# Decay levels of a gated linear recurrence: six levels in place of seven, products side by side in one bank, a compact matrix for the low levels

## The chip, the cores and the metric

The kernel runs on one core of a Trainium2 chip. The time is that of the device, in microseconds, from the launch on the core to its end; the median of several runs is compared. PE (TensorE) multiplies matrices and writes them to PSUM (8 banks, 512 fp32 columns of 128 partitions each); DVE (VectorE) and ACT (ScalarE) read and write PSUM and SBUF; POOL (GpSimd) works on SBUF alone; SP (SyncE) issues the DMAs. Each engine runs its own queue in order and waits on semaphores for the others.

## The reference

One decoder layer on x (1 x 1024 x 1024, fp32): RMSNorm, one input projection, two groups of token mixers (a gated linear recurrence and sliding-window attention), output projection into the residual, RMSNorm, SwiGLU FFN (1024 to 2816 to 1024). What the change touches is the recurrence, 4 heads of 128 key channels and 128 value channels:

```python
q = silu(q) * 128 ** -0.5;  f = lb + (1 - lb) * sigmoid(f_logit);  k = 1 - f;  logf = log(f)
def step(state, inp):                       # one chunk of tokens
    bcum = cumsum(gb, axis=2)               # decay sums, per channel
    diff = bcum[:, :, :, None, :] - bcum[:, :, None, :, :]
    decay = exp(where(causal, diff, NEG_INF))
    scores = einsum('bhtc,bhsc,bhtsc->bhts', qb, kb, decay)
    o_intra = einsum('bhts,bhsv->bhtv', scores, vb)
    o_inter = einsum('bhtc,bhcv->bhtv', qb * exp(bcum), state)
    btot = bcum[:, :, -1:, :]
    new_state = exp(btot[:, :, 0, :])[..., None] * state + einsum('bhsc,bhsv->bhcv', kb * exp(btot - bcum), vb)
    return new_state, o_intra + o_inter
o = rms_norm(o, out_gain) * silu(g)
```

The scores of a chunk carry a decay that depends on the channel, so they are no plain product of q and k.

## The kernel before

The tokens lie along the free dimension, channels on the partitions; a chunk is 128 tokens, 8 chunks (NC) a head. Projections and FFN are computed with each operand split in a high and a low part, three matmuls of 128x512 a step (the helper `three`, L1304 to L1306).

**The scores by levels.** The exponent b(t) - b(s) is written as (b(t) - m) - (b(s) - m), with m a decay sum between s and t, so that a product of q and k, each with its own factor, gives the score. One m doesn't serve all pairs, so there are 7 levels. At level lv, with L = 2^lv, a chunk falls into blocks of 2L tokens; m is the sum at the last token of the lower half; keys of the lower half meet queries of the upper half. Level 0 (L = 1) also gives the diagonal. A level goes through four engines:
- `LV` on POOL (L770): D = B - m, a subtraction of 128x1024; then `LV` on ACT (L1040, L1042 at level 0, else L1045 and L1046): the exponentials of both halves, in place
- `LX` on DVE (L1887): K times the factor, Q times the factor, into M, each 128x512 (L1875, L1878 at level 0, 128x1024 each)
- `LM` on PE (L1513): the products. Outputs are pieces of 32 partitions. Below 32 tokens only the four 32x32 pieces on a chunk's diagonal are computed (32 matmuls a level for the 8 chunks); at L = 32 there are 2 pieces of 32 columns a chunk, at L = 64 2 pieces of 64 columns. Each stands in PSUM at its place in the chunk's 128x128 score matrix, chunks 0 to 3 in bank 3, 4 to 7 in bank 4
- `LM` on DVE (L1897): two copies under a mask, 128x512 each, one a bank, that take what is valid at this level into the score matrix A (128 keys x 1024, fp32). The products of the next level wait for the copy of their bank

D and M have two buffers each, so `LV` of a level waits for the products two levels before, and `LX` for the matmuls two levels before.

Each matmul of fp32 shows as two records in the trace.

**Around the levels, per head.** `H1`: sigmoids and log on ACT. `HK`, `HQ`: K and Q on DVE. `HS` (L1854): the scan that gives the decay sums B. `H2`: exp(B) on ACT, its product with Q on POOL (L758), the tail difference on DVE (L1862) and its exponential on ACT; `HD` (L1867) multiplies it by K. `KT` (L1495): PE transposes that, into banks 3 and 4; `KE` on ACT copies it out. After the levels `OC`, chunk by chunk: a state product (L1528), the output product of A (L1530), the product with the state (L1533), and on DVE the state's update (L1906, L1910); ACT copies the outputs. `OS`, `OM`, `ON`, `OX` are the head's norm and gate. `W` (ACT, L942) and `WL` (DVE, L1739) split a projection weight tile in high and low; `MS`, `ML` split the input of the output projection.

**The order.** `schedule()` writes one list that all engines follow. `mix(dense, steps)` lays the steps of a head evenly between dense parts, each 6 matmuls of 128x512 of a projection. In head 0 there are 8 dense parts for the 7 levels, in heads 1 and 2 12 (2 more in head 2, of the output projection, for the last level), in head 3 16. Step lv of a head is `LM` of level lv, `LX` of lv + 2, `LV` of lv + 4.

## Time and profile before

| | us |
|---|---|
| median of 3 runs | 1136.88 (1135.83 to 1138.21) |
| the profiled execution | 1139.69 |
| its span, first to last instruction | 1138.0 |
| PE / DVE / ACT / POOL busy | 1093.1 / 699.3 / 497.3 / 439.4 |
| the four heads' levels and chunks | about 225 to 442 of the span |

The granted clock of TensorE is full (0.998 mean). A busy time counts the instructions' own time; the matmuls' ends are modelled and overlap, so that PE's rows are best read from start to start. An instruction's line names where it stands in the kernel; `x64` behind it counts records merged in one row. An idle time in brackets is the engine's own, just ahead of the instruction, with what ended it.

### The profile page before, as it was taken

How to read it: one execution, taken by the hardware profiler on the slowest of the kernel's cores; microseconds unless marked ns; L12 is line 12 of the kernel's file. 1: busy time of each engine (PE TensorE's matmuls, PEld its weight loads, DVE VectorE, ACT ScalarE, POOL GpSimd, SP SyncE). 2: the span in 40 equal slices, each digit the busy share in tenths (PEclk: the TensorE clock that was granted, in tenths of full speed). 3: DMA queues.
4: the chain of work that ended last, by engine and by line, in shares of the span. 5: the costliest groups of instructions: out<-in, count | busy, mean ns of one | idle time of the engine just before them, and what ended most of it. 6: DMA issues, size and time to landing. Idle time of an engine off the chain costs nothing.

```text
span 1138.0 us, 16737 instructions
## 1 busy us (share of the span) xinstructions
PE 1093.1 (96%) x6572; PEld 886.0 (78%) x6572; DVE 699.3 (61%) x884; ACT 497.3 (44%) x773; POOL 439.4 (39%) x351
## 2 busy tenths in 40 slices
PE   7999999979898999998999999999999999999998
PEld 7998766758676778776888888888888877788876
DVE  7205598596879897779332433243334497777776
ACT  8314466536456435454333333333333454454532
POOL 0301222354353332203646364536453844343462
PEclk9999999999999999999999999999999999999999
DMA  7101100010105104201333133313332594545333
GB/s 278 38 1 56 37 20 20 19 39 23 35 20 186 33 16 174 108 6 56 127 114 119 57 123 118 113 64 122 119 104 90 191 354 131 175 122 184 121 100 151
DMA packets 37102, 112.78 MB, mean 99 GB/s; under 512 B 4896, under 2 KB 9760, under 8 KB 35616
## 3 DMA queue, kind: packets, MB, share of 16 engines
q1 hardware_dynamic: 37024, 111.71, 28.5%
q8 instruction: 53, 0.87, 0.3%
q14 instruction: 25, 0.20, 0.1%
HBM read 83.12 MB, written 28.57 MB: 98 GB/s over the span
## 4 chain that ended last, share of the span: by engine, by line
PE 73%; DVE 12%; issue 5%; ACT 5%; POOL 3%; DMA 2%; SPq 0%; DVEq 0%; ACTq 0%; POOLq 0%
PE ps L1304 23%; PE ps L1306 22%; PE ps L1305 22%; DVE A L1897 2%; POOL D L770 1%; DMA ubraw<-hidden 1%; PE ps L1513 1%; DVE M L1887 1%; PE ps L1484 1%; PE ps L1321 1%; DVE B L1854 1%; DVE wlo L1739 1%; PE ps L1468 1%; DVE yacc L2038 0%; DVE sc L1812 0%
## 5 line engine op out<-in xcount | busy, mean ns | idle before, releaser
L1672 DVE TENSOR_TENSOR glo<-graw,ghi 128x1024 fp32r<-128x1024 f32 x21 | 26.2, 1246 | 148.2 <-POOL s34raw L680 147.2
L1304 PE MATMUL ps<-uhi,whi 128*128 128x512 f32 x272 | 112.8, 415 | 0.0
L1306 PE MATMUL ps<-uhi,wlo 128*128 128x512 f32 x272 | 106.4, 391 | 0.0
L1305 PE MATMUL ps<-ulo,whi 128*128 128x512 f32 x272 | 106.3, 391 | 0.0
L770 POOL TENSOR_TENSOR D<-B 128x1024 f32<-128x1024 f32 x28 | 64.3, 2295 | 41.4 <-DVE M L1887 22.0
L2038 DVE TENSOR_TENSOR yacc<-ps,yacc 128x512 f32<-128x512 f32 x104 | 68.7, 682 | 9.0 <-PE ps L1306 8.9
L1304 PE MATMUL ps<-ubhi,arhi 128*128 128x512 f32 x176 | 69.0, 392 | 2.3 <-DVE yacc L2038 2.2
L1304 PE MATMUL ps<-ohi,s12hi 128*128 128x512 f32 x168 | 66.3, 395 | 4.5 <-DVE olo L1705 2.7
L791 POOL TENSOR_TENSOR hst<-sg,up 128x512 f32<-128x512 f32 x21 | 29.5, 1404 | 103.0 <-issue 60.7
L1305 PE MATMUL ps<-ublo,arhi 128*128 128x512 f32 x176 | 68.5, 389 | 0.0
L1306 PE MATMUL ps<-ubhi,arlo 128*128 128x512 f32 x176 | 68.5, 389 | 0.0
L2006 DVE TENSOR_TENSOR ublo<-ubraw,ubhi 128x1024 fp32r<-128x1024 f32 (+1 forms) x44 | 51.7, 1181 | 24.8 <-ACT ubhi L1181 24.7
L1304 PE MATMUL ps<-ohi,s34hi 128*128 128x512 f32 x168 | 65.5, 390 | 0.8 <-ACT ps L1147 0.8
L1306 PE MATMUL ps<-ohi,s12lo 128*128 128x512 f32 x168 | 66.1, 393 | 0.0
L1305 PE MATMUL ps<-olo,s12hi 128*128 128x512 f32 x168 | 66.0, 393 | 0.0
L1305 PE MATMUL ps<-u2lo,ghi 128*128 128x512 f32 x168 | 65.4, 389 | 0.0
L1305 PE MATMUL ps<-olo,s34hi 128*128 128x512 f32 x168 | 65.4, 389 | 0.0
L1306 PE MATMUL ps<-ohi,s34lo 128*128 128x512 f32 x168 | 65.4, 389 | 0.0
L1304 PE MATMUL ps<-u2hi,ghi 128*128 128x512 f32 x168 | 65.4, 389 | 0.0
L1306 PE MATMUL ps<-u2hi,glo 128*128 128x512 f32 x168 | 65.4, 389 | 0.0
L1304 PEld LDWEIGHTS ps<-uhi,whi 128*128 128x128 f32 x272 | 51.1, 188 | 12.4 <-issue 0.9
L1306 PEld LDWEIGHTS ps<-uhi,wlo 128*128 128x128 f32 x272 | 51.1, 188 | 11.4
(323 smaller groups left out, 3010.1 us busy)
## 6 DMA issues: line engine op xcount, KB each, us to landing
hidden<-hst SPq DMA_DIRECT2D x11, 1792.0 KB, 6.0
ubraw<-hidden SPq DMA_DIRECT2D x33, 512.0 KB, 5.7
graw<-wg SPq DMA_DIRECT2D x21, 512.0 KB, 4.5
uraw<-wu SPq DMA_DIRECT2D x21, 512.0 KB, 3.5
wraw<-wproj SPq DMA_DIRECT2D x17, 512.0 KB, 3.6
araw<-wd SPq DMA_DIRECT2D x22, 384.0 KB, 4.9
x<-xT SPq DMA_DIRECT2D x8, 512.0 KB, 6.3
h<-xT SPq DMA_DIRECT2D x8, 512.0 KB, 4.7
```

Of the source, the lines that this page charges most:

```text
L770: nc.gpsimd.tensor_tensor(DD[lv % 2][:, :].rearrange("p (b l) -> p b l", l=2 * L), b4, mid, ALU.subtract).then_inc(s_lvs, 1)
L791: nc.gpsimd.tensor_tensor(hst[:, 4 if g % 2 else 7, :], sg2[:, :], upg[:, :], ALU.mult)\
L1304: nc.tensor.matmul(out, whi_, xhi_, start=first, stop=False, skip_group_check=seeded)
L1305: nc.tensor.matmul(out, whi_, xlo_, start=False, stop=False, skip_group_check=seeded)
L1306: return nc.tensor.matmul(out, wlo_, xhi_, start=False, stop=last, skip_group_check=seeded)
L1321: mm = nc.tensor.matmul(ps[:, 4 + x, :], ones[:, :], nsq[x][m][:, :], start=m == 0, stop=m == 7)
L1468: mm = nc.tensor.transpose(ps[:, 5 + i % 2, j * P:(j + 1) * P], sc[:, i % 3, j, :], ident[:, :])
L1484: mm = nc.tensor.matmul(ps[HD * g:HD * g + HD, 7, pair * 2 * P:(pair + 1) * 2 * P], vals, pT[:, t, g * 2 * P:(g + 1) * 2 * P], start=(t == ...
L1672: nc.vector.tensor_tensor((glo2 if g == 2 else glo[g % 2])[:, :], graw[g % 2][:, :], ghi[g % 2][:, :].bitcast(F32), ALU.subtract).then_inc ...
L1897: nc.vector.copy_predicated(av, lmask[:, lv, :].unsqueeze(1).broadcast_to([P, 4, P]), ps[:, 3 + x2, :].rearrange("p (c t) -> p c t", t=P))\
L2006: nc.vector.tensor_tensor(ublo[j % 3][i][:, :, :], ubraw[j % 3][i][:, :, :], ubhi[j % 3][i][:, :, :].bitcast(F32), ALU.subtract).then_inc( ...
L2038: nc.vector.tensor_tensor(yacc[q][:, t, :], ps[:, bank, :], yacc[q][:, t, :], ALU.add).then_inc(s_dadd, 1)
```

## The change

There are six levels, with L = 2, 4, ..., 64. Level 0 now takes groups of 4 tokens whole, diagonal in it, with m the mean of the decay sums at the group's second and third token; DVE works out these means behind the scan. A level's products lie side by side in one bank, chunk after chunk, even levels in bank 3 and odd ones in bank 4; only from level 2 on do the matmuls wait for a copy, that of two levels before. The four low levels are collected by one masked copy of 128x256 each in a compact matrix `near` (128 x 8 chunks x 32). ACT spreads `near` into A with four copies of 32 partitions when level 3 is in, copies level 4's products with two of 32 partitions and 256 columns, and level 5's with one of 64 partitions and 512 columns. What waited for the last masked copy now waits for ACT's last copy.

```diff
-LEVELS = 7
+LEVELS = 6
+BASE = 4
+SHORT = 4
+SPREAD = 7
 def level_size(lv):
-    return 1 << lv
+    return 2 << lv
...
-            steps[4] += [("OX", h - 1, 1)]
+            steps[3] += [("OX", h - 1, 1)]
...
-                for step in mix(take(n_p - taken[0]), steps[:6]):
+                for step in mix(take(n_p - taken[0]), steps[:LEVELS - 1]):
...
-                order += [("ML", 3)] + mix(take(TAIL), steps[6:])
+                order += [("ML", 3)] + mix(take(TAIL), steps[LEVELS - 1:])
...
+        smask = at("smask", 2.125, [P, SHORT, TILE], I8)
+        near = at("near", 1, [P, NC, TILE])
...
 POOL, setup: the masks of four levels, cut to 32 columns
+            for r in range(0, P, TILE):
+                step0(nc.gpsimd.tensor_copy(smask[r:r + TILE, :, :], lmask[r:r + TILE, :, r:r + TILE]))
...
 POOL, H1 of head 0
+                        pool.wait_ge(s_pte1, 2 * NC)
+                        nc.gpsimd.memset(near[:, :, :], 0.0).then_inc(s_setup, 1)
...
 POOL, LV
+                    if lv == 0:
+                        pool.wait_ge(s_mid, 2 * hh + 2)
+                        nc.gpsimd.tensor_tensor(DD[0][:, :].rearrange("p (b l) -> p b l", l=BASE),
+                                                B[:, :].rearrange("p (b l) -> p b l", l=BASE),
+                                                M[0][:, 0:T // BASE].unsqueeze(2).broadcast_to([P, T // BASE, BASE]),
+                                                ALU.subtract).then_inc(s_lvs, 1)
...
 ACT
+                elif kind == "LM" and step[2] >= SHORT:
+                    _, hh, lv = step
+                    A3 = A[:, :].rearrange("p (c t) -> p c t", t=P)
+                    if lv == SHORT:
+                        act.wait_ge(s_cp, SHORT * (hh + 1))
+                        act.wait_ge(*((s_oc, NC * hh) if hh else (s_setup, 3)))
+                        for r in range(0, P, TILE):
+                            nc.scalar.activation(A3[r:r + TILE, :, r:r + TILE], near[r:r + TILE, :, :], ACT.Copy)\
+                                .then_inc(s_sprd, 1)
+                    act.wait_ge(s_lmm, 2 * (LEVELS * hh + lv + 1))
+                    if lv == SHORT:
+                        for k in (0, 2 * TILE):
+                            far = ps[k:k + TILE, 3 + lv % 2, 0:NC * TILE].rearrange("p (c t) -> p c t", t=TILE)
+                            nc.scalar.activation(A3[k:k + TILE, :, k + TILE:k + 2 * TILE], far, ACT.Copy)\
+                                .then_inc(s_sprd, 1)
+                    else:
+                        far = ps[0:HD, 3 + lv % 2, :].rearrange("p (c t) -> p c t", t=HD)
+                        nc.scalar.activation(A3[0:HD, :, HD:P], far, ACT.Copy).then_inc(s_sprd, 1)
...
 PE, KT
-                        pe.wait_ge(s_cp, 14 * hh)
+                        pe.wait_ge(s_sprd, SPRD0 + SPREAD * hh)
...
 PE, LM
+                    if lv >= 2:
+                        pe.wait_ge(s_cp, SHORT * hh + lv - 1)
                     for c in range(NC):
-                        done = 2 * (7 * hh + lv - 1) + c // 4 + 1
-                        if c % 4 == 0 and lv:
-                            pe.wait_ge(s_cp, done)
                         for r, k0, q0, n in level_tiles(level_size(lv)):
                             at_k, at_q = c * P + k0, c * P + q0
-                            to = (c % 4) * P + q0
-                            mm = nc.tensor.matmul(ps[r:r + TILE, 3 + c // 4, to:to + n], lhs[:, at_k:at_k + TILE],
+                            mm = nc.tensor.matmul(ps[r:r + TILE, 3 + lv % 2, c * n:(c + 1) * n], lhs[:, at_k:at_k + TILE],
                                                   rhs[:, at_q:at_q + n], start=True, stop=True)
...
 PE, OC, chunk 0
-                        pe.wait_ge(s_cp, 14 * (hh + 1))
+                        pe.wait_ge(s_sprd, SPRD0 + SPREAD * (hh + 1))
...
 DVE, HS, behind the scan
+                    mid = M[0][:, 0:T // BASE]
+                    b4 = B[:, :].rearrange("p (b l) -> p b l", l=BASE)
+                    dve.wait_ge(*((s_lmm, 2 * LEVELS * hh) if hh else (s_tr, 2 * NC)))
+                    dve.wait_ge(s_scan, hh + 1)
+                    nc.vector.tensor_tensor(mid.unsqueeze(2), b4[:, :, 1:2], b4[:, :, 2:3], ALU.add).then_inc(s_mid, 1)
+                    dve.wait_ge(s_mid, 2 * hh + 1)
+                    nc.vector.tensor_scalar(mid, mid, 0.5, None, ALU.mult).then_inc(s_mid, 1)
...
 DVE, LM
-                    for x2 in range(2):
-                        dve.wait_ge(s_lmm, 2 * (7 * hh + lv) + x2 + 1)
-                        if lv:
-                            dve.wait_ge(s_cp, 2 * (7 * hh + lv - 1) + x2 + 1)
-                        av = A[:, x2 * HALF:(x2 + 1) * HALF].rearrange("p (c t) -> p c t", t=P)
-                        nc.vector.copy_predicated(av, lmask[:, lv, :].unsqueeze(1).broadcast_to([P, 4, P]),
-                                                  ps[:, 3 + x2, :].rearrange("p (c t) -> p c t", t=P))\
-                            .then_inc(s_cp, 1)
+                    dve.wait_ge(s_lmm, 2 * (LEVELS * hh + lv + 1))
+                    if lv == 0:
+                        dve.wait_ge(*((s_sprd, SPRD0 + SPREAD * hh) if hh else (s_setup, 4)))
+                    else:
+                        dve.wait_ge(s_cp, SHORT * hh + lv)
+                    nc.vector.copy_predicated(near[:, :, :], smask[:, lv, :].unsqueeze(1).broadcast_to([P, NC, TILE]),
+                                              ps[:, 3 + lv % 2, 0:NC * TILE].rearrange("p (c t) -> p c t", t=TILE))\
+                        .then_inc(s_cp, 1)
```

## Rows read from the trace of the kernel before

**Rows 1.** The page: busy time of each engine; shares of the last chain.
```profile
PE 1093.1 (96%) x6572; PEld 886.0 (78%) x6572; DVE 699.3 (61%) x884; ACT 497.3 (44%) x773; POOL 439.4 (39%) x351
...
PE 73%; DVE 12%; issue 5%; ACT 5%; POOL 3%; DMA 2%; SPq 0%; DVEq 0%; ACTq 0%; POOLq 0%
```

**Rows 2.** Windows: length, busy us (instructions) of PE, PEld, DVE, ACT, POOL; clock; DMA.
```profile
231.00:258.00 27.00, 23.07 (x453) 17.20 (x452) 25.92 (x32) 8.72 (x16) 13.17 (x6) 1.00 0.07 22
...
335.00:367.00 32.00, 28.11 (x463) 20.91 (x450) 30.98 (x40) 19.29 (x25) 11.48 (x6) 1.00 0.46 165
...
391.00:426.00 35.00, 33.64 (x503) 25.71 (x502) 34.68 (x43) 12.90 (x19) 12.63 (x6) 1.00 0.04 14
```

**Rows 3.** Timeline of PE, head 0: start, us, line, operation, [idle before <- releaser].
```profile
235.65 0.39 PE L1306 MATMUL ps<-uhi,wlo 128*128 128x512 f32 x1
235.97 0.76 PE L1513 MATMUL ps<-M,rec 128*32 128x32 f32 x64
236.66 0.50 PE L1304 MATMUL ps<-uhi,whi 128*128 128x512 f32 x1
...
243.95 0.40 PE L1306 MATMUL ps<-uhi,wlo 128*128 128x512 f32 x1
246.10 0.98 PE L1513 MATMUL ps<-M 128*32 128x32 f32 x64 [1.75 <-DVE A L1897]
247.02 0.50 PE L1304 MATMUL ps<-uhi,whi 128*128 128x512 f32 x1
```

**Rows 4.** Timeline of PE, the two upper levels of head 3.
```profile
418.43 0.39 PE L1306 MATMUL ps<-mhi,wlo 128*128 128x512 f32 x1
418.75 0.70 PE L1513 MATMUL ps<-M 128*32 128x32 f32 x32
419.38 0.50 PE L1304 MATMUL ps<-mhi,whi 128*128 128x512 f32 x1
...
422.32 1.09 PE L1513 MATMUL ps<-M 128*32 128x64 f32 x32
423.35 0.50 PE L1304 MATMUL ps<-mhi,whi 128*128 128x512 f32 x1
```

**Rows 5.** Timeline of PE, waits in heads 0, 1 and 2.
```profile
229.48 1.09 PE L1495 MATMUL ps<-ident,D 128*128 128x128 f32 x8 [1.99 <-DVE D L1867]
...
282.55 0.75 PE L1513 MATMUL ps<-M,rec 128*32 128x32 f32 x64 [0.74 <-ACT KDT L1031]
...
356.00 0.96 PE L1513 MATMUL ps<-M 128*32 128x32 f32 x32 [2.18 <-DVE A L1897]
...
363.53 0.50 PE L1304 MATMUL ps<-mhi,whi 128*128 128x512 f32 x1 [1.24 <-DVE mlo L1929]
...
370.02 0.49 PE L1533 MATMUL ps<-rec,S 128*128 128x128 f32 x2 [0.75 <-DVE S L1910]
```

**Rows 6.** Groups by line and shape: count, busy us, mean ns, idle before and releasers.
```profile
L770 POOL TENSOR_TENSOR D<-B 128x1024 f32<-128x1024 f32 x28 | 64.3, 2295 | 41.4 <-DVE M L1887 22.0 <-PE ps L1495 11.0 <-DVE rec L1878 8.0
...
L1897 DVE COPY_PREDICATED A<-lmask,ps 128x512 f32<-128x512 int8 x56 | 37.6, 723 | 0.5 <-PE ps L1513 0.5
...
L1887 DVE TENSOR_TENSOR M<-K,D 128x512 f32<-128x512 f32 x24 | 28.2, 1176 | 0.0
...
L1887 DVE TENSOR_TENSOR M<-Q,D 128x512 f32<-128x512 f32 x24 | 16.3, 679 | 0.0
...
L1045 ACT ACTIVATE D<-D 128x512 f32<-128x512 f32 x24 | 15.5, 644 | 41.4 <-POOL D L770 41.4
...
L1906 DVE SCALAR_TENSOR_TENSOR S<-S,small,ps 128x128 f32<-128x128 f32 x28 | 9.5, 340 | 8.6 <-PE ps L1528 8.5
```

**Rows 7.** Timeline of ACT, head 0.
```profile
222.52 0.20 ACT L1021 ACTIVATE small<-B 128x8 f32<-128x8 f32 x1
...
257.75 1.06 ACT L942 ACTIVATE whi<-wraw 128x1024 fp32r<-128x1024 f32 x1 [6.31 <-PE ps L1306]
```

**Rows 8.** Windows, from the end of the mixers to the end.
```profile
480.00:1138.00 658.00, 644.27 (x2802) 525.35 (x2800) 363.11 (x404) 262.70 (x354) 301.32 (x244) 1.00 0.36 126
```

More of the change, by code:

```diff
@@ L706, in _ @@
             step0(nc.gpsimd.memset(lmask[:, :, :], 0.0))
-            for lv in range(LEVELS):
-                L = 1 << lv
+            base = lmask[:, 0, :].rearrange("p (b l) -> p b l", l=BASE)
+            step0(nc.gpsimd.memset(lmask[:, 0, :], 1.0))
+            step0(nc.gpsimd.affine_select(out=base, in_=base, compare_op=ALU.is_ge, fill=0.0, base=0,
+                                          pattern=[[-BASE, P // BASE], [0, BASE]], channel_multiplier=1))
+            step0(nc.gpsimd.affine_select(out=lmask[:, 0, :], in_=lmask[:, 0, :], compare_op=ALU.is_ge, fill=0.0,
+                                          base=0, pattern=[[1, P]], channel_multiplier=-1))
+            for lv in range(1, SHORT):
+                L = 2 << lv
                 up = lmask[:, lv, :].rearrange("p (b u l) -> p b u l", u=2, l=L)[:, :, 1, :]
@@ L716, in _ @@
                                               pattern=[[2 * L, nb], [0, L]], channel_multiplier=-1))
-            step0(nc.gpsimd.affine_select(out=lmask[:, 0, :], in_=lmask[:, 0, :],
-                                          compare_op=ALU.not_equal, fill=1.0, base=0, pattern=[[-1, P]],
-                                          channel_multiplier=1))
+            for r in range(0, P, TILE):
+                step0(nc.gpsimd.tensor_copy(smask[r:r + TILE, :, :], lmask[r:r + TILE, :, r:r + TILE]))
             step0(nc.gpsimd.memset(scan_keep[:, :], 1.0))
@@ L737, in _ @@
                     pool.wait_ge(s_ass, 10)
-                    nc.gpsimd.memset(sc[:, 0:2, :, :], NEG).then_inc(s_neg, 1)
+                    nc.gpsimd.memset(sc[:, 0:2, :, :], NEG).then_inc(s_setup, 1)
                     pool.wait_ge(s_an, 5)
@@ L760, in _ @@
                     _, hh, lv = step
-                    L = 1 << lv
+                    L = 2 << lv
                     if lv == 0:
@@ L1803, in _ @@
                     if i == 0:
[L1804 to L1805 removed]
+                        dve.wait_ge(s_setup, 2)
                     if i >= 2:
@@ L1887, in _ @@
                         nc.vector.tensor_tensor(mv, sv, ev, ALU.mult).then_inc(s_lvm, 1)
[L1888 removed]
+                elif kind == "LM" and step[2] < SHORT:
                     _, hh, lv = step
[L1890 to L1899 removed]
+                    dve.wait_ge(s_lmm, 2 * (LEVELS * hh + lv + 1))
+                    if lv == 0:
+                        dve.wait_ge(*((s_sprd, SPRD0 + SPREAD * hh) if hh else (s_setup, 4)))
+                    else:
+                        dve.wait_ge(s_cp, SHORT * hh + lv)
+                    nc.vector.copy_predicated(near[:, :, :], smask[:, lv, :].unsqueeze(1).broadcast_to([P, NC, TILE]),
+                                              ps[:, 3 + lv % 2, 0:NC * TILE].rearrange("p (c t) -> p c t", t=TILE))\
+                        .then_inc(s_cp, 1)
                 elif kind == "OC":
```

49 lines of the change are left out of this document (23 added, 26 removed).

## The prediction, made before the changed kernel was run

> **What bounds the kernel now.** I read the page's busy times first: TensorE 96%, VectorE 61%, ScalarE 44%, GpSimd 39% [rows 1]. The chain that ended last is TensorE for 73% of the span and VectorE for 12% [rows 1]; that 12% says that somewhere the tensor queue runs on VectorE's time. The table of windows shows where: in the stretches of the decay levels VectorE is busy 25.9 of 27, 31.0 of 32 and 34.7 of 35 us, and TensorE only 23.1 of 27 and 28.1 of 32 [rows 2]. These are the stretches that the change touches.
>
> Then TensorE's timeline there. A projection matmul starts 0.23 us after the one before, so a level costs TensorE the time from 0.23 after the start of the last projection matmul to the start of the next. Level 0 of head 0: 235.65 + 0.23 = 235.88 to 236.66, 0.78 us, for 32 matmuls (64 records) with nothing late [rows 3]. Level 3 of the same head: 243.95 + 0.23 = 244.18 to 247.02, 2.84 us, with a wait for the masked copies into A (L1897), whose second half also splits the level in two [rows 3]. The two upper levels, 16 matmuls each, cost 418.66 to 419.38 = 0.72 us (32 columns) and, with the same lead before 422.32, 1.11 us to 423.35 (64 columns), when nothing is late [rows 4]. Read this way, the 28 levels (first and last in [rows 3, 4]) cost, from level 0 up:
> - head 0: 0.78, 1.30, 1.73, 2.84, 2.03, 1.02, 1.14 = 10.84
> - head 1: level 0 at 3.00 (with head 0's norm sums, L1539, in it; so too in heads 2 and 3, some 2.41 - 0.78 = 1.6), then 1.21, 0.78, 0.78, 2.02, 2.28, 1.67 = 8.74
> - head 2: 2.97, then 1.22, 0.78, 0.78, 0.78, 3.23, 2.42 = 9.21
> - head 3: 2.41, then 0.78, 2.22, 0.78, 0.78, 0.72, 1.11 = 6.39
>
> Undisturbed, six levels above level 0 are 4 x 0.78 + 0.72 + 1.11 = 4.95. So what is lost there is mostly waiting, and it is VectorE's: per head 14 copies of 0.723 us (10.1 us), then the products for the next levels [rows 6].
>
> **Part 1, one level less.** Six levels are 4 x 0.78 + 0.72 + 1.11 = 4.95 us of TensorE a head (level 0 in it) instead of 5.73: 0.78 a head, 3.1 in all, with no overlap to hide it since TensorE is the bound. VectorE loses 1.18 + 0.68 a head, ScalarE 2 x 0.64, GpSimd 2.3 [rows 6].
>
> The Trainium skill ("TensorE: Matmul & The Clock Gate", section "Wait — 56ns, not 53.3ns?") states that starts of matmuls never come closer than about 25 ns, however small they are. By it 64 records would be 1.6 us, and the four levels worth an estimated 6.4 us. The trace disagrees: 64 records from 235.97 to 236.66 are 10.8 ns each [rows 3], so the measurement decides.
>
> **Part 2, the copies.** VectorE's 14 copies of 128x512 become 4 of 128x256. No row has that shape; above it stands 0.723 (128x512, the same operation), below it 0.340 (128x128 out of PSUM) [rows 6]. A straight line gives 0.47, 1.9 us a head. ScalarE gets seven copies on 32 or 64 partitions: six of 256 elements, one of 512. Bounds 0.20 (8 elements) and 0.64 (512) [rows 6, 7]; the line gives 0.42 and 0.64, 3.2 us a head. They sit in ScalarE's queue ahead of the sigmoids of the next head. In head 0 ScalarE stands idle 6.31 us there, until TensorE has used a weight tile [rows 7], so they cost nothing; the first four need only level 3's copy and run while TensorE does levels 4 and 5, and the last (0.64 after level 5's products) has two dense parts of 1.4 us ahead of the chunk products in head 0, and the same or more in the others.
>
> VectorE per head then has about 8.2 + 1.9 us less to do. What is late next? In head 0 one dense part (1.50 us with the slower start behind a level) lies between levels, so TensorE wants a level every 2.28 us. A level also needs the ring: products on VectorE (1.4 beside GpSimd + 0.68), GpSimd's subtraction two levels on (1.9 to 2.9, mean 2.3), two exponentials (1.26), products again: 5.5 us for two levels, 2.75 for one. The schedule gives one extra dense part (1.37) between levels 3 and 4, so by placing the instructions one by one I get waits of 0.15, 0.25 and 0.25 on levels 3, 4 and 5: 0.7, where the bounds are 0 and 3. Heads 1 to 3 have two dense parts between most levels (3.65 us against 2.75): no wait.
> - head 0: 10.84 - (4.95 + 0.7) = 5.2 gained
> - head 1: 8.74 - 4.17 (five levels above level 0: 3 x 0.78 + 0.72 + 1.11) = 4.6
> - head 2: 9.21 - 4.17 = 5.0; the waits for the split output operand behind its last level (1.24 us [rows 5], counted in the 2.42, and some 0.3 at the next matmuls) shrink to 0.1: 5.3 in all. At its second chunk TensorE waits 0.75 for a state copy [rows 5], with its slower restart 1.0 us; VectorE comes late there behind the last copies. With them gone I count 1.0 more: 6.3
> - head 3: 6.39 - 4.17 = 2.2
>
> Sum 18.3.
>
> **Part 3, the block middles.** The two small VectorE instructions after each scan: bounds 0.34 and 0.68 each [rows 6], I take 0.4 each, 0.8 us. Behind them on VectorE's queue are a projection copy, a state update and the tail difference. In head 0 this leads over the exponential and L1867 to the transposes, where TensorE already waits 1.99 us [rows 5], so it can be 0.8 late. But L1867 there runs beside GpSimd's subtraction, and starts later into less of it: 0 to 0.8, I take 0.4. In heads 1 to 3 a state update comes 0.8 later and TensorE waits 0.4, 0.4 and 0.1; behind it stands a wait whose end ScalarE's queue sets (0.74 us at head 1's level 0 [rows 5], as much at head 2's), which takes most of it back: 0.5 left. GpSimd's level 0 waits for the middles but is held longer by its own product before it. The mask setup and the memset of the compact matrix lie where GpSimd has long idle times: nothing.
>
> **Sum.** 18.3 - 0.4 - 0.5 = 17.4 us. The profiled execution took 1139.69 (span 1138.0), so 1122.3, span 1120.6. The median of the runs is 1136.88, 2.8 below the profiled one; the same 17.4 gives 1119.5. It must carry to the end: from 480 us on TensorE is busy 644.3 of 658 us [rows 8], and what it waits for there is made from its own results, so all of it moves with it.
>
> **Rivals.**
> A. The ring of subtraction, exponential and products takes the copies' place. For: it is 2.75 us a level even with a free VectorE, and up to 3.2 if GpSimd takes 2.85 each time. Against: in three heads TensorE's step is longer. The Trainium skill ("GPSIMD Engine Reference", section "Specifications") speaks for it: GpSimd shares its SBUF interface with VectorE instructions that take two SBUF inputs. The copies read PSUM, and when they go the two-input products run closer behind each other against GpSimd. The trace agrees: the K products take 1176 ns and the Q products of the same shape, mostly after GpSimd has ended, 679 [rows 6]. Price: 2.5 in head 0 (3 - 0.7 and some), 1 in heads 1 and 2 each, 0.5 in head 3: 5 us, so 1124.5.
> B. Only work is saved, not waiting: the next late thing (weight splits, ScalarE behind TensorE, state updates) takes the room, or the second half gives it back. Then 3.1 plus the 0.23 us of the split in a dozen levels: some 6 us, 1131. Against: the waits name the copies; the second half's idle time is 14 us in all and belongs to TensorE's own results.
> C. The change does nothing that can be measured: as B, with the middles at 0.68 and their waits given in full (0.8 + 3 x 1.2, 4.4 us): 1135.
> D. Slower: writing a level's products side by side makes TensorE's small matmuls queue. It pays where a level of 64 records takes over 1.5 us, since 24 levels x 0.73 is the 17.4: 23 ns a record instead of 10.8. At 40 ns a level is 2.6, the 16 short levels cost 16 x 1.9 = 30 more, 1149. For: the level whose 32 records fall on two of the four row groups of PSUM takes 0.63 for half the records [rows 4], so pace does depend on where outputs go. Against: the row groups stay as they are, only columns move.
>
> **Chances.** Forecast 0.71, A 0.15, B 0.09, C 0.02, D 0.03. Faster by over 0.2% (2.3 us, about what a measurement of this kernel can tell from no change): 0.95; same 0.02; slower 0.03. The forecast's own range is 1115 (all waits in head 0 gone, the 0.9 of part 3 not paid and some more of the other waits gone: 17.4 + 0.7 + 0.9 + 1.5 = 20.5, and 1.4 for the runs' spread) to 1124; taking in A and the half of B brings the top to 1127.
>
> **What would show it.** Right: records at L1513's successor 1280 instead of 1536, the four short levels at 0.78 with no split; VectorE's copies 16 at about 0.47; TensorE's waits for them nearly gone in heads 1 to 3, little in head 0; the levels' stretch of head 0 shorter by 5, of head 2 by 6; the time from the last level to the end unchanged. Wrong: waits of 0.5 us or more on the products or on GpSimd at each level (A); chunk 0 waiting for ScalarE's copies; the stretch after 480 us longer (B); a short level well over 0.8 without a wait (D).

## The result, and the profile after

The changed kernel takes 1125.24 us (median of 4 runs, 1123.18 to 1125.52), the kernel before in the same series 1137.12: a ratio of 0.9886, with a 95% interval of 0.9872 to 0.99, or 11.9 us less. The forecast was 17.4 us less, 1119.5, with a range of its own of 1115 to 1124; the measured time lies above that and inside the 1127 that took in a part of the rivals. The changed kernel's profiled execution took 1125.46, 0.2 above its median; that of before lay 2.8 above its own. So in the traces the difference is larger, 14.3 us of span (1138.0 to 1123.7), and that is the number that rows can explain.

The page of the kernel after, busy time and last chain, to set beside [rows 1]:

```profile
PE 1089.1 (97%) x6316; PEld 883.1 (79%) x6316; DVE 681.5 (61%) x844; ACT 504.1 (45%) x793; POOL 425.2 (38%) x342
...
PE 79%; DVE 9%; issue 4%; ACT 4%; DMA 2%; POOL 1%; SPq 0%; DVEq 0%; ACTq 0%; POOLq 0%
```

VectorE's share of the chain that ended last fell from 12 to 9%, not to nothing. Windows tell where the time went. First the kernel after, from 200 us to the end of the mixers, and from there to the end (length; busy us of PE, PEld, DVE, ACT, POOL):

```profile
200.00:428.70 228.70, 219.55 (x2235) 173.98 (x2234) 175.39 (x203) 124.88 (x179) 76.44 (x36) 0.99 0.17 58
428.70:1123.70 695.00, 681.68 (x2955) 553.21 (x2953) 392.13 (x446) 280.48 (x380) 312.76 (x251) 1.00 0.36 125
```

The same second stretch in the kernel before:

```profile
442.40:1138.00 695.60, 681.78 (x2955) 553.88 (x2953) 393.80 (x446) 280.63 (x380) 313.14 (x251) 1.00 0.36 125
```

695.0 against 695.6 us: the second half gave nothing back. All of the gain is in the four heads (242.4 us before, 228.7 after).

TensorE's timeline of head 0 after, levels 0, 1 and 4, and level 5 of head 3, answers to [rows 3, 4]:

```profile
238.29 0.39 PE L1345 MATMUL ps<-uhi,wlo 128*128 128x512 f32 x1
238.61 0.76 PE L1550 MATMUL ps<-M,rec 128*32 128x32 f32 x64
239.31 0.50 PE L1343 MATMUL ps<-uhi,whi 128*128 128x512 f32 x1
...
240.57 0.40 PE L1345 MATMUL ps<-uhi,wlo 128*128 128x512 f32 x1
240.90 0.76 PE L1550 MATMUL ps<-M 128*32 128x32 f32 x64
241.59 0.50 PE L1343 MATMUL ps<-uhi,whi 128*128 128x512 f32 x1
...
408.31 0.39 PE L1345 MATMUL ps<-mhi,wlo 128*128 128x512 f32 x1
408.62 1.09 PE L1550 MATMUL ps<-M 128*32 128x64 f32 x32
409.64 0.50 PE L1343 MATMUL ps<-mhi,whi 128*128 128x512 f32 x1
```

A level of 64 records costs 238.29 + 0.23 = 238.52 to 239.31, 0.79 us, as before. No level is split by a wait for the matrix any more. Counted in the prediction's way (from 0.23 us after the start of the last dense matmul to the start of the next), TensorE's blocks in us are as follows. The row of the levels holds all levels in head 0, and those above level 0 in heads 1 to 3:

| block | before | after | after, no means |
|---|---|---|---|
| transposes KT(0) | 3.00 | 4.17 | 3.00 |
| levels head 0 / 1 / 2 / 3 | 10.84 / 8.74 / 9.21 / 6.39 | 5.63 / 4.17 / 4.18 / 4.18 | 6.89 / 4.16 / 4.17 / 4.17 |
| chunks (OC) head 0 / 1 / 2 | 4.98 / 4.71 / 5.47 | 7.02 / 7.04 / 6.29 | 4.69 / 4.69 / 5.80 |
| level 0 of head 1 / 2 / 3 | 3.00 / 2.97 / 2.41 | 2.20 / 2.20 / 2.41 | 2.97 / 3.00 / 2.21 |
| transposes KT(3) | 3.23 | 1.41 | 3.65 |
| sum | 64.95 | 50.90 | 49.40 |

64.95 - 50.90 = 14.05. The levels gained 17.0. The chunks lost 5.2 and KT(0) 1.2; the blocks behind them gave back 3.4. (The third column is an experiment below.)

The table holds only blocks, and one more loss stands between them. Right behind the wait at KT(0) TensorE's projection matmuls start 0.43 us apart, eight times, where they start 0.23 us apart before and after that:

```profile
231.84 0.63 PE L1344 MATMUL ps<-ulo,whi 128*128 128x512 f32 x1
232.27 0.63 PE L1345 MATMUL ps<-uhi,wlo 128*128 128x512 f32 x1
```

The granted clock is the reason: from 231.4 to 235.0 us it is 0.53 of full on average, and at its low point 0.50 (1.2 instead of 2.4 GHz), for 3.4 us; just before, TensorE had waited 3.16 us. Such a stretch is called a half clock below. In the same place the kernel before, after a wait of 1.99 us, has 1.00. The loss is 1.6 us, and no row of the table has it. The account is then: 14.05 by the blocks, 1.1 between them (there are four blocks fewer, and a restart behind a block is slower; 0.4 of it lies behind head 2's last level, where a wait for the split operand is gone), less 1.6 of the clock, and 0.7 outside the heads: the span's 14.3.

What the chunks wait for stands in TensorE's timeline after, at the transposes and at the sixth and seventh chunk of head 0. The first row answers to the first of [rows 5]:

```profile
230.52 1.10 PE L1534 MATMUL ps<-ident,D 128*128 128x128 f32 x8 [3.16 <-DVE D L1910]
...
268.64 0.49 PE L1570 MATMUL ps<-rec,S 128*128 128x128 f32 x2 [0.56 <-DVE S L1947]
...
272.19 0.49 PE L1570 MATMUL ps<-rec,S 128*128 128x128 f32 x2 [1.23 <-DVE S L1947]
```

TensorE waits for VectorE's state update S. Among the chunks it did so for 0.25 us in head 0 and 0.75 in head 2 in the kernel before. VectorE's queue shows why. The kernel after, behind the scan of head 0:

```profile
219.09 2.28 DVE L1890 TENSOR_TENSOR_SCAN B<-scan_keep,B 128x1024 f32<-128x1024 bf16 x1
221.48 0.63 DVE L1896 TENSOR_TENSOR M<-B 128x256 f32<-128x256 f32 x1
222.14 0.29 DVE L1898 TENSOR_SCALAR M<-M 128x256 f32<-128x256 f32 x1
222.35 0.68 DVE L1807 TENSOR_TENSOR rawf<-ps,rs 128x512 f32<-128x512 f32 x1
222.95 3.08 DVE L1905 TENSOR_TENSOR D<-B 128x1024 f32<-128x1024 f32 x1
```

and GpSimd in that time:

```profile
222.55 2.40 POOL L772 TENSOR_TENSOR rec<-Q,D 128x1024 f32<-128x1024 f32 x1 [7.39 <-ACT D L1039]
```

The kernel before, the same two engines:

```profile
221.43 0.66 DVE L1770 TENSOR_TENSOR rawf<-ps,rs 128x512 f32<-128x512 f32 x1
222.02 1.22 DVE L1862 TENSOR_TENSOR D<-B 128x1024 f32<-128x1024 f32 x1
...
222.69 2.82 POOL L758 TENSOR_TENSOR rec<-Q,D 128x1024 f32<-128x1024 f32 x1 [7.40 <-ACT D L1018]
```

The two instructions for the means take 0.63 + 0.29 = 0.92 us. With them the tail difference D = B(end of chunk) - B starts at 222.95 instead of 222.02. Before, it started 0.67 us ahead of GpSimd's product Q exp(B) and took 1.22; now it starts 0.40 us behind that product's start and takes 3.08. In the four heads it starts 0.08 to 0.65 us behind and takes 2.80 to 3.39. The groups by line and shape of the kernel after have the mean, 3143 ns (count, busy us, mean ns):

```profile
L1930 DVE TENSOR_TENSOR M<-K,D 128x512 f32<-128x512 f32 x20 | 32.6, 1628 | 0.0
L1930 DVE TENSOR_TENSOR M<-Q,D 128x512 f32<-128x512 f32 x20 | 13.6, 678 | 0.0
L1905 DVE TENSOR_TENSOR D<-B 128x1024 f32<-128x1024 f32 x4 | 12.6, 3143 | 0.0
L1550 PE MATMUL ps<-M 128*32 128x32 f32 x896 | 12.0, 199 | 0.5 <-DVE M L1930 0.4
L1938 DVE COPY_PREDICATED near<-smask,ps 128x256 f32<-128x256 int8 x16 | 7.0, 438 | 0.2 <-PE ps L1550 0.2
L1075 ACT ACTIVATE A<-near 32x256 f32<-32x256 f32 x16 | 6.6, 414 | 3.2 <-DVE near L1938 2.9
```

beside this of the kernel before:

```profile
L1862 DVE TENSOR_TENSOR D<-B 128x1024 f32<-128x1024 f32 x4 | 4.9, 1217 | 0.0
```

So 0.92 us of new work became 0.92 + 1.93 = 2.85 us a head on VectorE's queue, with the state updates behind it. The Trainium skill ("GPSIMD Engine Reference", section "Specifications") says that GpSimd contends for its SBUF interfaces with VectorE instructions in a two-port performance mode or with two SBUF inputs; this trace agrees (1.22 us became 3.08 for an instruction with two SBUF inputs). Experiment 2 below has one with a single SBUF input that is stretched too; whether it ran in such a mode no run here shows. Also to be read above: the copies cost what the straight lines gave (438 ns for an estimated 0.47 us; 414 for 0.42), and the K products rose from 1176 [rows 6] to 1628 ns.

### The profile page after: what moved, and what is told of

It reads as the page before. It is cut to its first block, busy times and chain, and to the rows that moved or that the text cites. A ratio compares the mean times of both kernels' runs of the same rounds, so it can differ in the third digit from the quotient of the medians.

```text
span 1123.7 us, 16159 instructions
## 1 busy us (share of the span) xinstructions
PE 1089.1 (97%) x6316; PEld 883.1 (79%) x6316; DVE 681.5 (61%) x844; ACT 504.1 (45%) x793; POOL 425.2 (38%) x342
## 4 chain that ended last, share of the span: by engine, by line
PE 79%; DVE 9%; issue 4%; ACT 4%; DMA 2%; POOL 1%; SPq 0%; DVEq 0%; ACTq 0%; POOLq 0%
PE ps L1343 25%; PE ps L1344 24%; PE ps L1345 24%; PE ps L1550 2%; DMA ubraw<-hidden 1%; PE ps L1523 1%; DVE B L1890 1%; PE ps L1360 1%; PE ps L1507 1%; DVE D L1905 1%; PE ps L1576 1%; DVE yacc L2079 0%; DVE sc L1848 0%; DVE smax L1852 0%; PE ps L1493 0%
## 5 line engine op out<-in xcount | busy, mean ns | idle before, releaser
L680 POOL TENSOR_TENSOR s12raw<-uraw 128x512 f32<-128x512 f32 x21 | 27.9, 1330 | 83.2 <-DVE h L2124 46.6
```

What stands on the lines that cost most here:

```text
L680: nc.gpsimd.tensor_tensor(sw[:, 0:HALF], uw[:, 0:HALF], uw[:, HALF:D], ALU.add).then_inc(s_sum, 1)
```

## The experiments

Two theories for the missing gain. T1: the missing gain is the means, by the instruction behind them that now collides with GpSimd. T2: it is the rival A of the prediction, the ring of subtraction, exponential and products, or another chain that comes into view once the copies are gone. All experiments were made in three series, each with runs of the kernel before beside them (medians 1136.87, 1137.05, 1138.10).

**1. No means.** Level 0 takes the decay sum at the second token of its group instead of the mean of the second and third.

```diff
-    nc.vector.tensor_tensor(mid.unsqueeze(2), b4[:, :, 1:2], b4[:, :, 2:3], ALU.add)
-    nc.vector.tensor_scalar(mid, mid, 0.5, None, ALU.mult)
 # GpSimd, level 0
-    M[0][:, 0:T // BASE].unsqueeze(2).broadcast_to([P, T // BASE, BASE])
+    b4[:, :, 1:2].broadcast_to([P, T // BASE, BASE])
```

> The changed kernel without the two small VectorE instructions of the block means: level 0 takes the decay sum at its group's second token as m, so the scores are the same but for rounding. Theory 1 (position): the means cost little by themselves (0.63 + 0.29 us), but they push the tail difference behind them into GpSimd's product, where it takes 3.1 us instead of 1.22, and that late queue makes TensorE wait for state updates (1.4 and 2.1 us instead of 0.6 each) and for the first transposes (4.17 instead of 3.00). Without them: tail difference 1.22 again, those waits as in the kernel before, level 0 of heads 1 and 2 back from 2.20 to 3.0, transposes of head 3 back from 1.41 to 3.2; in sum 4.0 us faster than the changed kernel, 1121.2. Theory 2 (own time): only the 0.92 us counts, where nothing covers it, in head 0: 1.0 us faster, 1124.2.

Measured: 1123.36 (1120.3 to 1123.6), ratio 0.9872 (0.9855 to 0.9888); 1.9 us below the kernel after, against the 4 or 1 expected (1.6 by the two ratios, whose intervals overlap; the spans differ by 2.2). The groups of this kernel:

```profile
L1897 DVE TENSOR_TENSOR D<-B 128x1024 f32<-128x1024 f32 x4 | 4.9, 1216 | 0.0
```

and TensorE's timeline, two of the three late levels of head 0, and KT(3):

```profile
243.94 0.76 PE L1549 MATMUL ps<-M 128*32 128x32 f32 x64 [0.82 <-DVE M L1922]
...
248.00 0.70 PE L1549 MATMUL ps<-M 128*32 128x32 f32 x32 [0.35 <-DVE M L1922]
...
376.11 1.06 PE L1533 MATMUL ps<-ident,D 128*128 128x128 f32 x8 [2.68 <-DVE S L1939]
```

The collision is gone, and with it every wait of the chunks of heads 0 and 1: T1's mechanism holds. Its size does not, since other waits come out from under it (third column of the table): levels 2 and 3 of head 0 now wait for the products (T2's ring, 1.26 us in the block), the first chunk of head 2 waits 1.07 us for ScalarE's last copy, KT(3) is at 3.65 again. The 6.3 us that came back in KT(0) and the chunks (1.17 + 2.33 + 2.35 + 0.49) became 1.5 net by the table. The half clock moved as well: behind KT(0), with a wait of 1.99 us, it is gone, and it stands behind KT(3) and its wait of 2.68 us instead, at the same price of 1.6.

**2. The tail difference first.** The means stay, but behind the tail difference.

```diff
+    nc.vector.tensor_tensor(dv, bc[:, :, P - 1:P].broadcast_to([P, NC, P]), bc, ALU.subtract)
     nc.vector.tensor_tensor(mid.unsqueeze(2), b4[:, :, 1:2], b4[:, :, 2:3], ALU.add)
     nc.vector.tensor_scalar(mid, mid, 0.5, None, ALU.mult)
```

> The changed kernel with the tail difference put right behind the scan, ahead of the means. Theory 1: the tail difference starts before GpSimd's product and takes 1.22 us; the add of the means has two SBUF inputs and takes its place beside the product, 0.63 grows to 1.5 to 2.5; the transposes of head 0 are back at 3.0 us or below, the state update behind the means is late once instead of twice: 1 to 3 us faster than the changed kernel, 1123. Theory 2: the same instructions in another order, no difference (1125), or slower, as the state update comes 1.2 us later.

Measured: 1133.79 (1133.36 to 1135.48), ratio 0.9974 (0.9964 to 0.9985). A clear miss of the 1123 that T1 gave; its theory 2 allowed for slower, without a size. VectorE's timeline of this kernel:

```profile
221.16 1.23 DVE L1896 TENSOR_TENSOR D<-B 128x1024 f32<-128x1024 f32 x1
222.30 0.62 DVE L1902 TENSOR_TENSOR M<-B 128x256 f32<-128x256 f32 x1
222.95 2.39 DVE L1904 TENSOR_SCALAR M<-M 128x256 f32<-128x256 f32 x1
225.26 0.68 DVE L1807 TENSOR_TENSOR rawf<-ps,rs 128x512 f32<-128x512 f32 x1
225.86 2.72 DVE L1776 TENSOR_TENSOR wlo<-wraw,whi 128x1024 fp32r<-128x1024 f32 x1
```

The tail difference is at 1.23 us as T1 wanted, but now the multiplication by 0.5, which took 0.29 us in the kernel after, stands beside GpSimd's product (222.29 to 225.18) and takes 2.39. It ends with that product, as if it could not go on while GpSimd ran. The addition, which T1 expected to be stretched, took its 0.62 us. The queue is as late as before and the weight split behind it is late too (2.72 us beside GpSimd's next operation), so that TensorE's timeline has in head 0:

```profile
270.97 0.49 PE L1570 MATMUL ps<-rec,S 128*128 128x128 f32 x2 [3.64 <-DVE S L1947]
```

So it is in heads 1 and 2 (3.62 and 3.77 us). Behind each of these three waits the granted clock falls to 0.50 for 3.4 us. The blocks sum to 56.6 us, 5.7 above the kernel after, and the three half clocks add 2.8 between them, 8.5 together, where the spans differ by 8.2. Some instruction stands beside the product in both orders; what matters is which.

**3. The product waits.** GpSimd's product starts only when the tail difference has ended.

```diff
+    pool.wait_ge(s_d2, hh + 1)
     nc.gpsimd.tensor_tensor(qi(hh), Q[:, :], DD[0][:, :], ALU.mult).then_inc(s_qi, 1)
```

> The changed kernel with one wait more: GpSimd's product of Q and exp(B) starts only when the tail difference is done. Theory 1: no overlap, so the tail difference takes 1.22 us although the means are where they were; the waits for state updates shrink to some 0.4 us beyond the 0.6 each; GpSimd starts 1.3 us later and its level 0 ends as much later, which has some 3 us of slack ahead of the transposes in heads 1 to 3 but not in head 0: 1.5 to 2.5 us faster than the changed kernel, 1123. Rival: the tail difference is slow for another reason (what the means do to it on VectorE itself, its operands), stays at 3.1 and the time is 1125 or more.

Measured: 1129.03 (1127.75 to 1130.15), ratio 0.9927 (0.9915 to 0.994), a miss by 6 us. Its rival is refuted: the tail difference is at 1220 ns, and each chunk stretch of heads 0 and 1 falls from 7.0 to 5.5 us. But GpSimd's own chain is the longer one. TensorE's timeline of this kernel, KT(0) and level 0 of head 1:

```profile
231.18 1.09 PE L1535 MATMUL ps<-ident,D 128*128 128x128 f32 x8 [3.48 <-DVE D L1911]
...
281.85 0.75 PE L1551 MATMUL ps<-M,rec 128*32 128x32 f32 x64 [1.54 <-ACT KDT L1053]
```

Level 0 of heads 1 and 2 rises from 2.20 to 3.79 and 3.73, KT(3) from 1.41 to 4.98: the product is followed by level 0's subtraction and ScalarE's exponentials, ahead of ScalarE's copies of the transposes. The expectation gave this chain some 3 us of slack in heads 1 to 3. That slack is GpSimd's (3.33 us idle before its next subtraction in head 1 of the kernel after); ScalarE's copies of the transposes in head 1 start 2.28 us later than in the kernel after (280.64 for 278.36).

**4. The means alone**, added to the kernel before, and not used by its levels.

```diff
     nc.vector.tensor_tensor_scan(B[:, :], ...)
+    nc.vector.tensor_tensor(mid.unsqueeze(2), b4[:, :, 1:2], b4[:, :, 2:3], ALU.add)
+    nc.vector.tensor_scalar(mid, mid, 0.5, None, ALU.mult)
```

> The kernel before with the two instructions of the means added behind each scan, and nothing that uses them. Theory 1: the tail difference grows from 1.22 to 3.1 us, state updates and first transposes late as in the changed kernel, part of it given back at level 0 and in head 3: 4.0 us slower than before, 1141. Theory 2: 1 us slower, 1138.

Measured: 1140.86 (1137.78 to 1142.95), ratio 1.0029 (1.0011 to 1.0046), that is 1.3 to 5.2 us slower. The groups of this kernel have the collision without the rest of the change:

```profile
L1870 DVE TENSOR_TENSOR D<-B 128x1024 f32<-128x1024 f32 x4 | 12.6, 3160 | 0.0
```

Its chunks of heads 0 and 1 cost 7.29 and 7.02 us, like those of the kernel after. In the trace the span grew by only 0.4, since the levels behind took most of it back, 2.9 us shorter (32.3 for 35.2). But these are spans, and the parts outside the heads differ between the two executions: up to KT(0) this one was 0.9 us ahead, and behind the mixers it gained 0.9 more. From KT(0) to the end of the mixers it took 217.5 us for 215.3, so 2.2 more: 0.5 by the blocks and 2.4 by two half clocks that the kernel before does not have there (behind KT(0), and behind a wait of 2.25 us in head 2), less 0.7 between the blocks. The mechanism is shown; its price here is 2.2 us in the heads by the traces, and 1.3 to 5.2 by the runs.

**5 and 6. Each half of the change alone.** Six levels with the old masked copies of whole banks, and seven levels with the compact matrix and ScalarE's copies; neither has the means.

```diff
 # 5, against the kernel before
-LEVELS = 7
+LEVELS = 6
-    return 1 << lv
+    return 2 << lv
 # 6, against the kernel after without means
-LEVELS = 6
-SHORT = 4
+LEVELS = 7
+SHORT = 5
-    return 2 << lv
+    return 1 << lv
```

> The kernel before with six levels in place of seven and nothing else: the products still go to two banks, VectorE still copies all of them under masks into the full matrix, and level 0 takes the decay sum at the second token of its group, without the two instructions for the mean. Theory 1 (a level costs its matmuls and, while the copies bind, the wait for them too): the level blocks of before come to 10.84, 8.74, 9.21 and 6.39 us for six levels after level 0, so one level less is worth 1.8 + 1.5 + 1.5 + 1.1 = 5.9 us: about 1131. Theory 2 (a level costs its matmuls alone, 0.78 us a head, and the waits for VectorE stay whole): 3.1 us: about 1133.8.

> The kernel after with seven levels in place of six, without the means: products side by side, compact matrix, ScalarE spreads it and copies the two upper levels. Theory 1 (the copies are the larger part, and each level then costs its 64 matmuls, 0.78 us): 13.5 us of the kernel without means, less 4 levels at 0.78 = 3.1: about 10.4 us below before, 1126.5, with no wait of TensorE for the matrix in any level. Theory 2 (the ring of subtraction, exponential and products binds once the copies are gone, and with seven levels in it at every level of head 0): some 4 us more, 1130 to 1131, with waits on M at most levels of head 0.

Measured: five, 1127.04 (1126.07 to 1128.14), ratio 0.9913 (0.9899 to 0.9926), 10.0 us faster, a miss of both its theories. Six, 1129.02 (1128.48 to 1130.08), ratio 0.9932 (0.992 to 0.9944), 8.0 faster, between its two. Head 0 in TensorE's timeline of the first:

```profile
245.84 0.99 PE L1517 MATMUL ps<-M 128*32 128x32 f32 x64 [1.71 <-DVE A L1901]
```

and of the second:

```profile
248.37 0.76 PE L1541 MATMUL ps<-M 128*32 128x32 f32 x64 [1.74 <-DVE M L1914]
```

The 35.2 us of level blocks fall to 24.2 with one level less, to 25.0 with the copies alone, to 19.4 with both. One level less is worth 11.0 us of blocks alone and 5.6 on top of the copies; the copies 10.2 alone and 4.8 on top of the shorter ladder. Both take the same waits away: 18.0 us in the two medians, 13.5 together (17.6 and 14.6 by the ratios, so that the blocks, 21.2 against 15.8, are the firmer evidence). In the first, six levels on VectorE's old queue still wait for the matrix; in the second the copies are gone, the K products take 1738 ns instead of 1176, and the wait is for the products: A's ring, with seven levels in it, as its theory 2 said (two of the three waits of head 0 over 0.8 us). The level's worth was beyond theory 1's 5.9 us too. An estimate says why: a level takes 2 x 0.72 + 1.18 + 0.68 = 3.3 us of VectorE and 0.78 of TensorE, and the 11.0 us are 2.75 a head, so a level taken out of a queue that is behind gives back nearer to its share of VectorE than to its matmuls.

**7. Another order, no means.** In head 2, ScalarE copies level 5 ahead of the weights that it waits for, and VectorE takes the last state update ahead of the remainders (ML) of the output's operand.

```diff
-    steps[6] += [("ML", 4), ("MS", 5)]
-    steps[7] += [("ML", 5)]
+    steps[6] += [("MS", 5)]
+    steps[7] += [("ML", 4), ("ML", 5)]
+    i = order.index(("LM", h, LEVELS - 1))          # head 2 only: W, LM -> LM, W
+    order[i - 1:i + 1] = order[i - 1:i + 1][::-1]
```

> The kernel without means with two changes in the order of head 2: ScalarE copies level 5 before it splits the weights that it waits for from a DMA, and VectorE takes the last state update of head 2 before the remainders of the output's operand, which wait for ScalarE. Theory 1 (the waits of 1.07 us in front of the first output chunk and of 2.2 of the 2.68 us at the transposes of head 3 are only the order's): 3 us less than without means (1123.4): about 1120.3, and the block of the transposes falls from 3.65 to about 1.4 us. Theory 2 (they wait for GpSimd's and ScalarE's chain of head 3 anyway, and the work in front only covers it): 1123, with the waits at the next block.

Measured: 1122.88 (1122.35 to 1123.03), ratio 0.9875 (0.9862 to 0.9889): no change from experiment 1 that can be told, theory 2. KT(3) fell from 3.65 to 0.79, and the next block of TensorE's timeline had the wait:

```profile
380.60 0.76 PE L1552 MATMUL ps<-M,rec 128*32 128x32 f32 x64 [2.55 <-DVE rec L1916]
```

VectorE now did the remainders (4.06 us, beside GpSimd) ahead of level 0's products of head 3. The medians hide a part, though. From KT(0) to the end of the mixers this trace is 2.9 us shorter than that of experiment 1 (197.1 for 200.0): 1.5 by the blocks, and the half clock behind KT(3) is gone with its wait. It then has two half clocks behind the mixers where that of experiment 1 has none, and starts KT(0) 0.8 us later.

**8. ScalarE's spreads twice**, in the kernel after.

```diff
-    for r in range(0, P, TILE):
+    for r in (*range(0, P, TILE), *range(0, P, TILE)):   # the second time behind the first
```

> The kernel after with the four copies by which ScalarE spreads the compact matrix done twice in each head, the second time behind the first (1.74 us more of ScalarE a head). Theory 1 (ScalarE's copies are hidden: it waits for TensorE, 0.9 us before its next weights in head 0, and the first output chunk starts 2.0 us after the last copy ended): within 0.5 us of the kernel after, 1125.2 to 1125.8, no wait for the matrix at the first output chunk but in head 2 at most. Theory 2 (they are on the path): 1.7 us for each of three or four heads, 1130 to 1132.

Measured: 1126.84 (1124.68 to 1127.72), ratio 0.9906 (0.9891 to 0.9921), 1.6 us above the kernel after (2.3 by the ratios) for 7 us more of ScalarE. ScalarE's timeline of this kernel in head 0:

```profile
250.07 3.50 ACT L1079 ACTIVATE A<-near 32x256 f32<-32x256 f32 x8 [0.95 <-DVE near L1942]
253.60 0.77 ACT L1085 ACTIVATE A<-ps 32x256 f32<-32x256 f32 x2
254.39 0.59 ACT L1089 ACTIVATE A<-ps 64x512 f32<-64x512 f32 x1
255.01 1.06 ACT L963 ACTIVATE whi<-wraw 128x1024 fp32r<-128x1024 f32 x1
```

No chunk 0 waits for the matrix in any head. The weights that follow start 4.94 us behind the first spread where it was 4.06: of 1.75 us, 0.9 were idle time. The other 0.9 go on in head 0 over ScalarE's logarithm and VectorE's queue (which waits 3.05 us for it where it was 2.19) to one more wait of TensorE for S, 0.82 us. And in head 2 ScalarE rounds a part of the output's operand behind the spreads, VectorE's remainder waits for that, and TensorE for the remainder:

```profile
355.72 0.50 PE L1347 MATMUL ps<-mhi,whi 128*128 128x512 f32 x1 [0.84 <-DVE mlo L1974]
```

The kernel after has neither wait, and they come to the 1.6. So the spreads do not delay the first output chunk, as theory 1 said, but they are not hidden whole, and its 0.5 us was exceeded.

**9 and 10. More of the order, without and with the means.** In head 2 the remainders and their roundings (MS) also go behind the transposes' copies and level 0's products of head 3; in heads 0 to 2 ScalarE copies the transposes (KE) before it squares the head's output (OS). The tenth is the kernel after with the same order.

```diff
-    steps = [[("OC", h, c)] for c in range(NC)] + [[("OS", h)]]
+    steps = [[("OC", h, c)] for c in range(NC)] + [[]]
-    steps += [[("KE", h + 1), ("LV", h + 1, 1), ("LV", h + 1, 2)]]
+    steps += [[("KE", h + 1), ("OS", h), ("LV", h + 1, 1), ("LV", h + 1, 2)]]
 # head 2
+    steps[9] = [("KE", h + 1), ("OS", h), ("LV", h + 1, 1), ("MS", 4), ("ML", 4),
+                ("LV", h + 1, 2), ("MS", 5), ("ML", 5)]
```

> The reordered kernel without means, with three more moves: in head 2 VectorE's two remainders of the output's operand and ScalarE's two roundings go behind the transposes, the first products and ScalarE's copies of head 3, and in heads 0 to 2 ScalarE copies the transposes before it squares the head's output. Theory 1 (LM0(3) waited 2.55 us for products that stood behind the remainders, LM0(1) and LM0(2) 0.74 for copies that stood behind the squares): 2.2 + 0.6 + 0.6 us off the 1122.9 of the reordered kernel, about 1119.5; blocks of level 0 at 2.2 to 2.4 us in every head. Theory 2 (GpSimd's and ScalarE's chain into the next head binds whatever the order is): 1122 to 1123, the waits at the next level.

> The kernel after, with its means, in the same order as the kernel before this one in the list. Theory 1 (with the means the state updates are late on VectorE by the tail difference, 3.1 us beside GpSimd's product, and nothing of it depends on this order; the waits that the order takes away were covered by it): 0 to 1 us below the kernel after, 1124.3 to 1125.2; the means then cost 5 us of this order. Theory 2 (the order alone is worth 3 us, with the means or without): 1122.

Measured: without the means 1118.33 (1118.11 to 1122.24), ratio 0.9835 (0.9816 to 0.9855); with them 1125.51 (1125.07 to 1127.27), ratio 0.9895 (0.9878 to 0.9911). The order is worth 5.0 us without the means (4.2 by the ratios to before) and nothing with them. Level 0 of head 3 in TensorE's timeline of the ninth has no wait, a smaller one has come at the next level:

```profile
376.19 0.76 PE L1550 MATMUL ps<-M,rec 128*32 128x32 f32 x64
...
383.32 0.76 PE L1550 MATMUL ps<-M 128*32 128x32 f32 x64 [1.71 <-DVE M L1923]
```

and the tenth has that wait too (1.71), and besides still those of the kernel after in heads 0 and 1:

```profile
272.36 0.49 PE L1571 MATMUL ps<-rec,S 128*128 128x128 f32 x2 [1.24 <-DVE S L1948]
```

The ninth is the fastest kernel here, 6.9 us below the kernel after (5.8 by the ratios). Its blocks sum to 45.9 us, 3.5 below experiment 1, where the medians differ by 5.0. Its profiled execution was the slowest of its four (1122.24), and the granted clock goes with that: 0.995 on average, with a half clock of 3.4 us behind the wait just shown and one of 6.8 us from 500 us on, against 0.998 in the other three (1118.1 to 1118.4). The tenth's blocks sum to 51.2, where those of the kernel after sum to 50.9: what its order took away at KT(3) and in head 2's chunks (0.6 each) came again at head 3's level 1 (1.8).

## Why the prediction was right, and where its size was off

The direction, the mechanism in the levels and its size there were right; the term for the means was not. The point was 5.7 us too low, and the time fell outside the forecast's own 1115 to 1124. It lies in the wider range only because the top was set to 1127 for A and a part of B; neither came in that form, so that much is luck.

- **Part 1 and the price of a level: right.** 0.79 us for 64 records, 0.72 and 1.10 for the upper levels, 1280 records. D is refuted: side by side, the records queue no more than before. But its worth as a term of its own was not additive: alone it brought 10.0 us, not 3.1. In the sum this made no difference, since part 2 counted the waits from the levels' whole cost.
- **Part 2, levels: right head by head.** Forecast 5.2, 4.6, 5.0, 2.2; measured 5.2, 4.6, 5.0, 2.2 (17.0). Head 0's residual waits were to be 0.15, 0.25, 0.25; there was one of 0.35, and slower restarts. That it was so little is partly luck: without the means the ring costs 1.3 more. There the time from KT(0) to level 0 is 2.8 us shorter (8.55 for 11.32), which leaves GpSimd and ScalarE less time to run ahead; that this is the reason is argued, not tested. The ring's own sum has a slip, 1.4 + 0.68 + 2.3 + 1.26 is 5.6, not 5.5, and its 1.4 was 1.63 in the kernel after.
- **Part 2, the rest of head 2: right too, under a new loss.** Of the 1.3 us (0.3 + 1.0), the matmuls behind its last level gave 0.4, and the second chunk's wait went (its block 1.60 to 0.59). Two new waits for S, at the sixth and eighth chunk, cover it in the table. So part 2 brought 18.4 us for the 18.3 forecast.
- **Part 2, ScalarE's copies hidden: right in heads 0, 1 and 3**, where even doubled spreads do not delay the first chunk (experiment 8). In head 2 it holds only while other things are late: without the means the first chunk there waits 1.07 us for ScalarE's last copy, which was among the signs of being wrong.
- **Part 3 is the term that was mis-sized.** It had 0.92 us of new work right (0.8), and the queue behind it right, and then priced the tail difference at its old 1.22 us. Measured, it took 3.14. At TensorE: KT(0) +1.17 (forecast +0.4), chunks of heads 0, 1 and 2 +2.04, +2.33, +1.83 (+0.4, +0.4, +0.1; the last is the +0.82 of the table and the 1.01 that the second chunk gave), given back 3.4 at level 0 of heads 1 and 2 and at KT(3). Net 4.0. On top come 1.6 us of half clock behind KT(0), a term that the sum did not have at all. Together 5.6 us for 0.9 forecast. With 18.4 of part 2 and 1.5 that were not in the sum (0.7 between the blocks, 0.7 outside the heads), 18.4 - 5.6 + 1.5 = 14.3, the span's difference.
- **The half clock at KT(0) goes with the means** in all kernels: the six with means have it at KT(0), where TensorE waited 2.69 to 3.48 us, and the six without, the kernel before among them, don't, with waits of 1.97 to 1.99. Taking the means out did not give all of that back (1.9 us in experiment 1), since other waits and another half clock stood beneath; in the order of experiments 9 and 10 the means cost 7.2. The rows that would have told it were there: the tail difference ended 0.55 us after the product's start, 0.9 us of delay puts it wholly behind that start, and VectorE's two-input instructions beside GpSimd took 1176 against 679 ns [rows 6].
- **The rest, 14.3 in the spans against 11.9 in the medians,** is the frame: I took a gain worked out from one execution off the median of others. No row stands for the 2.4 us.
- **B and C are refuted** by the second half (695.0 us against 695.6) and the levels. B's late state updates did come, but through the means: without them heads 0 and 1 have no such wait. **A** was not what held the kernel after, where the levels cost what was forecast; its time (1124.5) came out near by another cause. It is real beneath: 1.26 us in head 0 without the means, and the bound of the copies-only kernel.

## What to carry to other kernels

A small instruction put in front of others costs more than its time if it pushes one of them to start behind an instruction of GpSimd that it then has to share with: before adding work to VectorE's queue, look up what runs on GpSimd one such delay later, and price what then stands beside it at the rate of rows that did collide. After a longer wait of TensorE, read the granted clock of the stretch behind it too: a table of waits does not show what a half clock costs. Gains that come out of one queue's waits don't add (10.0 and 8.0 us apart, 13.5 together), so add up what is left, and not what each removes alone. And after a wait has been removed, look again at the order: the same reordering was worth 4 to 5 us once the late instruction was gone and nothing while it was there.

## What the runs showed of the hardware

- Which of two colliding instructions is stretched depends on which starts first. A 128x1024 subtraction on VectorE takes 1.22 us alone, and also when GpSimd's product starts while it runs; then the product takes longer, the more the earlier it starts: 3.08 us when it starts 0.42 behind the subtraction, 2.82 at 0.67, 2.46 at 1.01 (the kernel before). When the product starts first it takes 2.38 to 2.40, and the subtraction 2.80 to 3.39: it ended 1.07 to 1.09 us after the product in all four heads (226.03 - 224.95 = 1.08 in head 0), as if it had begun when that ended. Why this is so no run here shows.
- A 128x256 multiplication by a constant, one SBUF operand, took 0.29 us alone and 2.35 us on average beside GpSimd (experiment 2, 4 times); it, too, ended with the product. The 128x256 addition of strided columns, two SBUF operands, took 0.62 us in the same place, where it started 0.01 us behind the product, and there the product took 2.83 to 2.89. Which of the two was first, the rows don't settle.
- A masked copy of 128x256 out of PSUM took 438 ns and a ScalarE copy of 32 partitions x 256 414 ns: both lie within 0.03 us of the straight line between rows with fewer and with more elements in a partition, the second although it has 32 partitions and those rows 128.
- The granted clock of TensorE fell to 0.50 (1.2 GHz) for 3.4 us behind the waits of 2.68 to 3.77 us that the traces have in the heads. The length of one wait does not tell it: the clock fell behind 1.74 us in experiment 6 (head 0) and behind 2.25 in experiment 4 (head 2), and not behind 2.25 at the kernel before's KT(3) or 2.55 in experiment 7; behind 1.71 us at head 3's level 1 it fell in experiment 9 and not in experiment 10. At 0.50 the starts of 128x512 matmuls are 0.43 us apart instead of 0.23, so that a half clock of 3.4 us costs 1.6 where TensorE has work throughout.
